# One more 128-column product ahead of each 256-column stretch of the feed-forwards

## The chip, the cores and the metric

The kernel runs on one core of a Trainium2 chip. The metric is the device time of one execution in microseconds, the median of several runs. TensorE (PE in the profile) multiplies; its weight loads have a row of their own (PEld). VectorE is DVE, ScalarE is ACT, GpSimd is POOL, and SyncE (SP) issues the large loads.

## What is computed

Two blocks over 256 tokens of width 1024, batch 1. The first has two layers (a gated mixer with a feed-forward, then an attention over compressed, selected and near tokens with a feed-forward); the second block has a gated linear attention with a convolution and a feed-forward with a convolution over a grid. Each has its own modulation from a condition. What bears on the change are the three feed-forwards:

```python
# first block, layers 0 and 1: ff_w_in is 1024 x 4096, ff_w_out 4096 x 1024
h = modulate(rms_norm(x, norm_g[layer, 2]), sh2, sc2)
y = jnp.square(jax.nn.relu(h @ ff_w_in[layer])) @ ff_w_out[layer]
x = x + g2[:, None, :] * rms_norm(y, norm_g[layer, 3])
...
# second block: w_up is 1024 x 5632, w_down 2816 x 1024
u, gate = jnp.split(h @ w_up, 2, axis=-1)
u = dwconv_grid(u, w_cf, b_cf, rows, width)
return (jax.nn.silu(u) * gate) @ w_down
```

All weights and activations are float32.

## The kernel before

The kernel is written engine by engine, with semaphores set by hand; the order of PE's work is the order of the calls in its program. Every weight matrix is streamed in chunks of 128 x 2048 float32 (1 MB) through a ring of six buffers (`raw`). A chunk is split into two tiles in the rounded float32 format: ACT writes the high part (`whi`, L724), DVE the rest (`wlo`, L1199), in rings of three. Activations are split the same way: `hh` and `hl` are the two halves of `hcat`. A product of the exact numbers is then three products of rounded ones: high by high, high by low and low by high. A rounded product is one record on PE; a product of plain float32 tiles (the full format) is two records, two passes. The trace writes f32 for both.

There are two kinds of stretches on PE in a feed-forward. `feature_major` (L1963) takes a chunk of 256 output features by 1024 inputs: for each half of 128 features and each of 8 slices of the inputs it issues the three products (L1971, L1972, L1973), the weights being the stationary operand and 256 tokens the moving one. That is 48 products of 256 columns into one bank; `linear_mid` (L2017) waits for the chunk (`split_ready`) and for the bank (`mid_free`) and calls it. `rows_onto_y` (L2056) takes a chunk of 256 rows of the output matrix: `tile_onto_y` (L2030) issues products with the activations stationary and 512 columns of the weights moving (L2039), 24 of them, into four banks that hold the sum over all chunks.

`ffn` (L2082) runs the two feed-forwards of the first block: first `ff_in(0)`, through `first_product`, which follows the normalised input slice by slice; then for c from 0 to 14 `ff_in(c + 1)` and, up to c = 13, `rows_onto_y` of chunk c; `end_of_y` ends it. In between stand a few products for the modulation (`ada_sum`, `ada_cols`, `ctx_transposes`, `ada_chunks`, `gain_row`). The last feed-forward has an up and a gate chunk in each step: `up(M_UP[c + 1])` and `up(M_GA[c + 1])`, 96 products of 256 columns, then `down(c)`, 24 products of 512. Other parts use `linear_mid` as well, the GLA part between products of the attention levels (L2520).

Each product has a weight load of its own, which PE can run while the product before it streams.

Of the kernel before, what the change touches and what calls it, by code (L numbers as in the profile page):

```python
# [11 lines left out]
P = 128  # L12
# [74 lines left out]
def build(nc, I, out, upto="ffn2"):  # L87
# [154 lines left out]
    if has("ffn2"):  # L242
# [3 lines left out]
        M_UP, M_GA, M_DN = [0] * CF, [0] * CF, [0] * CF  # L246
# [33 lines left out]
    hh, hl = hcat[:, :, 0, :], hcat[:, :, 1, :]  # L280
# [187 lines left out]
    ps = [banks[:, 512 * i:512 * i + 512] for i in range(8)]  # L468
# [9 lines left out]
    def sem(name):  # L478
        if name not in sems:
            sems[name] = nc.alloc_semaphore(name)  # L480
        return sems[name]

    raw_full = [sem(f"raw_full{i}") for i in range(RAW)]
    s_hi, s_lo, s_mm = sem("hi_ready"), sem("lo_ready"), sem("chunk_multiplied")
# [141 lines left out]
    with block:  # L626
# [1223 lines left out]
        def _(pe):  # L1850
# [106 lines left out]
            def w_of(m, kts=KT):  # L1957
                w = pl.width[m] // kts
                v = slice(0, pl.width[m])
                return (whi[:, m % SPL, v].rearrange("p (k n) -> p k n", n=w),  # L1960
                        wlo[:, m % SPL, v].rearrange("p (k n) -> p k n", n=w))

            def feature_major(m, bank, ah, al, between=None):  # L1963
                wh, wl = w_of(m)
                for nt in range(wh.shape[2] // P):
                    if nt and between is not None:
                        between()
                    dst = bank[:, T * nt:T * nt + T]
                    n = slice(nt * P, nt * P + P)
                    for kt in range(KT):  # L1970
                        pe.matmul(dst, wh[:, kt, n], ah[:, kt, :], start=kt == 0, stop=False)  # L1971
                        pe.matmul(dst, wh[:, kt, n], al[:, kt, :], start=False, stop=False)  # L1972
                        mm = pe.matmul(dst, wl[:, kt, n], ah[:, kt, :], start=False, stop=kt == KT - 1)  # L1973
                return mm
# [35 lines left out]
            def split_ready(m):  # L2010
                pe.wait_ge(s_lo, m + 1)
# [2 lines left out]
                if pl.last_use(pl.bank[u], u):  # L2014
                    pe.wait_ge(s_mid, pl.last_use(pl.bank[u], u))

            def linear_mid(m, ah, al, tm=False, o=None, between=None):  # L2017
                u = pl.um[m]
                split_ready(m)
                mid_free(u)  # L2020
                bank = ps[pl.bank[u]]
                if o is not None:
                    mm = first_product(m, bank, ah, al, o, tm)
                elif tm:
                    mm = token_major(m, bank, ah, al)
                else:
                    mm = feature_major(m, bank, ah, al, between)
                mm.then_inc(s_mm, 1)

            def tile_onto_y(m, ah, al, t, first=False):  # L2030
# [51 lines left out]
            def ffn(f, o, u, meanwhile=dummies, first=lambda: None):  # L2082
                m0, c0 = M_FF[f], 16 * f
                u0 = pl.um[m0]
                def ff_in(c, o=None):
                    linear_mid(m0 + (2 * c - 1 if c else 0), hh, hl, o=o)

                def squares(c):
                    pe.wait_ge(s_fact, c0 + c + 1)
                    at_ = lambda b: (lambda k, s: b[:, c % 3, T * k + s.start:T * k + s.stop])  # L2090
                    return at_(fhi), at_(flo)

                boundary(2 * f + 1, meanwhile, first)
                ff_in(0, o=o)
                if f == 1:
                    ada_cols(S2)
                for c in range(15):
                    if c == 14:

                        pe.wait_ge(s_gain, 2 * u + 1)  # L2100
                    ff_in(c + 1)
                    if ends_at(f, c - 1) is not None:
                        ada_sum(ends_at(f, c - 1))
                    if c + 1 in CTX_STEPS and f == 1 and has("gla"):
                        ctx_transposes(CTX_STEPS.index(c + 1))
                    if c >= 13:

                        pe.wait_ge(s_mid, u0 + c)
                        gain_row(u, c - 13)
                    if c < 14:  # L2110
                        rows_onto_y(m0 + 2 * c + 2, *squares(c), first=c == 0)
                        ada_chunks(FF_ADA[f][c])
                        if ends_at(f, c - 1) is not None:
                            ada_cols(ends_at(f, c - 1))

                def squares_ready():
                    pe.wait_ge(s_fact, c0 + 16)
                    if f == 1 and has("gla"):

                        pe.wait_ge(s_t, 8 * 6)  # L2120
                    ada_sum(ends_at(f, 14))

                r14 = squares(14)
                at_ = lambda b: (lambda k, s: b[:, 15 % 3, T * k + s.start:T * k + s.stop])
                end_of_y(m0 + 30, r14, (at_(fhi), at_(flo)), squares_ready, lambda: ada_cols(ends_at(f, 14)))
                ada_chunks(FF_ADA[f][14])
# [51 lines left out]
            if has("gmlp"):  # L2178
# [22 lines left out]
                for j in range(4):  # L2201
# [3 lines left out]
                    if j == 0:  # L2205
# [3 lines left out]
                        for b in range(2):  # L2209
                            for q in range(4):  # L2210
                                mm = pe.transpose(ps[b][:, q * P:q * P + P], ws[:, 4 * b + q, :], ident[:, :])
# [33 lines left out]
            if has("attn"):  # L2245
# [12 lines left out]
                for j in range(2):  # L2258
                    pe.wait_ge(s_blk, j + 1)
                    for c in range(2):  # L2260
                        m = M_CW[j][c]
                        split_ready(m)
                        wh, wl = w_of(m)
                        for i in range(8):
                            k = (8 * c + i) * WIN
                            ah, al = bw[j][:, k:k + P], bw[j][:, 16 * WIN + k:16 * WIN + k + P]
                            pe.matmul(ps[j][:, 0:T], ah, wh[:, i, :], start=c == 0 and i == 0, stop=False)
                            pe.matmul(ps[j][:, 0:T], ah, wl[:, i, :], start=False, stop=False)
                            mm = pe.matmul(ps[j][:, 0:T], al, wh[:, i, :], start=False, stop=c == 1 and i == 7)
                        mm.then_inc(s_mm, 1)  # L2270
                linear_mid(M_Q[1], hh, hl)
                for j in range(2):
                    pe.wait_ge(s_ht, j + 1)
                    for nt in range(2):
                        mm = pe.transpose(ps[2 + j][:, WIN * nt:WIN * nt + WIN], ht[:, j, P * nt:P * nt + P], ident[0:WIN, 0:WIN])
# [5 lines left out]
                wh, wl = w_of(M_GT)  # L2281
                for kt in range(KT):
# [3 lines left out]
                    mm = pe.matmul(dst, wl[:, kt, :], hh[:, kt, :], start=False, stop=kt == KT - 1)  # L2286
# [5 lines left out]
                for g in range(NG):  # L2292
                    for nt in range(2):
                        for i in range(2):
                            mm = pe.matmul(ps[1][32 * i:32 * i + NC, HD * g:HD * g + HD], hid[:, 1, nt, NC * g:NC * g + NC], w2v[:, nt, :],
                                           start=nt == 0, stop=nt == 1)
# [3 lines left out]
                for t in range(2):  # L2300
                    mm = pe.transpose(ps[4][:, 48 * t:48 * t + 48], gate_fm[:, P * t:P * t + P], ident[0:48, 0:48])
# [113 lines left out]
            if has("gla"):  # L2415
# [60 lines left out]
                for j in range(4):  # L2476
                    mm = pe.matmul(ps[2 + j // 2][:, T * (j % 2):T * (j % 2) + T], wab2[:, P * j:P * j + P], alx[:, :], start=True, stop=True)
# [16 lines left out]
                for f in range(2):  # L2494
                    for pair in range(GHD // 2):
                        for tt in range(2):
                            for h in (2 * pair, 2 * pair + 1):
                                dst = ps[2][64 * (h % 2):64 * (h % 2) + 64, 256 * f + P * pair:256 * f + P * pair + P]
                                mm = pe.matmul(dst, wc[:, tt, 256 * f + 64 * h:256 * f + 64 * h + 64], vctx[:, tt, P * h:P * h + P],
                                               start=tt == 0, stop=tt == 1)  # L2500
# [36 lines left out]
                for pair in range(GHD // 2):  # L2537
# [5 lines left out]
                    for h in (2 * pair, 2 * pair + 1):  # L2543
                        for it in range(2):
                            for jt in range(2):
                                a_ = (a_d if it == jt else a_x)[:, h % 2, jt, pair, :]
                                mm = pe.matmul(o_of(h)[:, P * it:P * it + P], vx[:, jt, P * h:P * h + P], a_, start=False, stop=it + jt == 2)
# [30 lines left out]
            if has("ffn2"):  # L2578
                def last_modulation(e):

                    pe.wait_ge(s_l4, 2)
                    pe.wait_ge(s_msr, 2)
                    ada_chunks(4)

                boundary(5, last_modulation)

                def up(m, bank, o=None):
                    split_ready(m)
                    if o is None:
                        feature_major(m, ps[bank], hh, hl).then_inc(s_mm, 1)  # L2590
                    else:
                        first_product(m, ps[bank], hh, hl, o).then_inc(s_mm, 1)

                def down(c):
                    pe.wait_ge(s_cact, c + 1)
                    at_ = lambda b: (lambda k, s: b[:, c % 2, T * k + s.start:T * k + s.stop])
                    if c < CF - 1:
                        rows_onto_y(M_DN[c], at_(chi), at_(clo), first=c == 0)
                    else:
                        last_rows_onto_y(M_DN[c], at_(chi), at_(clo))  # L2600

                up(M_UP[0], 6, o=7)
                ada_cols(G2B)
                up(M_GA[0], 4)
                for c in range(CF):
                    if c + 1 < CF:
                        if c:
                            pe.wait_ge(s_ue, c)
                        else:

                            ada_bank_free(G2B + 1)
                        up(M_UP[c + 1], 6 + (c + 1) % 2)
                        if c:
                            pe.wait_ge(s_fa, c)
                        up(M_GA[c + 1], 4 + (c + 1) % 2)
                    else:

                        pe.wait_ge(s_ue, c)
                        pe.wait_ge(s_fa, c)
                        gain_row(U_FF2, 0)  # L2620
                        gain_row(U_FF2, 1)
                    down(c)
# [119 lines left out]
```

## Time and profile before

| | |
|---|---|
| median of 3 runs | 1011.76 us (1010.94 to 1012.22) |
| the profiled execution | 1011.14 us |
| its span, first to last instruction | 1009.2 us |
| PE busy | 983.7 us, 6900 products |
| PE's weight loads busy | 865.8 us, 6901 loads |
| DVE busy | 801.6 us |
| ACT busy | 539.9 us |
| POOL busy | 77.4 us |
| read from HBM | 239.37 MB, 238 GB/s over the span |

A start is exact to the nanosecond in the records and printed to 0.01 us in the timeline. The end of a product is modelled, and products overlap: one of 256 columns is recorded as some 280 ns long though the next one starts well under 120 ns after it. So the pace of a stretch is read from the starts: the start of a product late in it less the start of an early one, by the number of steps between them. In the timeline neighbouring records of one line with the same operands are merged into one row (x2, x4).

### The profile page before, as it was taken

What the parts mean: (1) busy time and instruction counts of PE and PEld (TensorE: products, weight loads), DVE (VectorE), ACT (ScalarE), POOL (GpSimd) and SP (SyncE); (2) the same over time, 40 slices, a digit from 0 to 9 for tenths busy, and PEclk for the clock granted to TensorE, in tenths of its full rate; (3) what the DMA queues carried; (4) which work ended last, traced back from release to release, by engine and by line L of the source; (5) the groups of instructions that cost most, each with busy time, mean ns of one, the idle gap of its engine ahead of it and who ended that gap; (6) DMA issues with size and microseconds to landing.
All of it is one profiled execution on the core that took longest, in us unless ns stands there. A gap on an engine that the chain in (4) does not pass through costs nothing.

```text
span 1009.2 us, 16926 instructions
## 1 busy us (share of the span) xinstructions
PE 983.7 (97%) x6900; PEld 865.8 (86%) x6901; DVE 801.6 (79%) x1208; ACT 539.9 (53%) x706; POOL 77.4 (8%) x80
## 2 busy tenths in 40 slices
PE   6999999999999999999999999999999999999997
PEld 3687799989987989887889999988998889999996
DVE  2449799858988988877979778873799789888896
ACT  4354554444446547775545455464765765454544
POOL 0000000000000000000540000000791000000000
PEclk9999999999999999999999999999999999999999
DMA  9999699969997999002998877735433386555511
GB/s 340 387 384 375 224 337 393 349 225 358 351 338 255 287 365 353 2 2 84 377 372 299 282 269 286 255 95 167 127 132 127 119 282 220 186 189 190 186 43 42
DMA packets 130332, 243.60 MB, mean 241 GB/s; under 512 B 6586, under 2 KB 95311, under 8 KB 124111
## 3 DMA queue, kind: packets, MB, share of 16 engines
q1 hardware_dynamic: 125616, 238.77, 66.9%
q10 hardware_dynamic: 4639, 3.76, 1.4%
q8 instruction: 54, 0.88, 0.4%
q14 instruction: 23, 0.19, 0.1%
HBM read 239.37 MB, written 1.05 MB: 238 GB/s over the span
## 4 chain that ended last, share of the span: by engine, by line
PE 76%; DVE 6%; DMA 5%; POOL 4%; ACT 4%; SPq 2%; issue 2%; POOLq 0%; DVEq 0%; ACTq 0%
PE bank L2039 26%; PE bank L1971 11%; PE bank L1973 11%; PE bank L1972 11%; PE bank L2051 3%; DMA raw<-in_a_w_in_dram 3%; DVE wlo L1199 2%; DMA raw<-in_cmp_w_dram 1%; PE bank L2324 1%; PE bank L2350 1%; SPq L654 1%; DMA raw<-in_b_w_in_dram 1%; ACT whi L724 1%; PE bank L1865 1%; PE bank L2362 1%
## 5 line engine op out<-in xcount | busy, mean ns | idle before, releaser
L1199 DVE TENSOR_TENSOR wlo<-raw,whi 128x2048 fp32r<-128x2048 f32 x143 | 327.3, 2295 | 47.3 <-ACT whi L724 46.2
L724 ACT ACTIVATE whi<-raw 128x2048 fp32r<-128x2048 f32 x144 | 274.3, 1905 | 144.6 <-PE bank L2039 76.6
L1971 PE MATMUL bank<-hcat,whi 128*128 128x256 f32 x1096 | 309.1, 282 | 2.3 <-DVE wlo L1199 1.9
L1972 PE MATMUL bank<-hcat,whi 128*128 128x256 f32 x1096 | 307.0, 280 | 0.0
L1973 PE MATMUL bank<-hcat,wlo 128*128 128x256 f32 x1096 | 306.9, 280 | 0.0
L1971 PEld LDWEIGHTS bank<-hcat,whi 128*128 128x128 f32 x1096 | 206.0, 188 | 9.1 <-issue 3.5
L1973 PEld LDWEIGHTS bank<-hcat,wlo 128*128 128x128 f32 x1096 | 208.9, 191 | 0.0
L1972 PEld LDWEIGHTS bank<-hcat,whi 128*128 128x128 f32 x1096 | 206.0, 188 | 1.4
L1818 DVE SCALAR_TENSOR_TENSOR cvt<-ut,vec,cvt 128x189 f32<-128x189 f32 (+2 forms) x176 | 68.2, 429 | 19.3 <-ACT cvt L1162 16.8
L2039 PE MATMUL bank<-whi,fhi 128*128 128x512 f32 x240 | 74.7, 392 | 0.0
L2039 PE MATMUL bank<-wlo,fhi 128*128 128x512 f32 x240 | 74.0, 390 | 0.0
L2039 PE MATMUL bank<-whi,flo 128*128 128x512 f32 x240 | 74.0, 389 | 0.0
L859 ACT ACTIVATE fr<-bank 128x512 f32<-128x512 f32 x32 | 19.1, 598 | 95.4 <-PE bank L1973 91.3
L1237 DVE SCALAR_TENSOR_TENSOR acc_wide<-raw,csil,acc_wide 128x2048 f32<-128x2048 f32 x28 | 65.6, 2344 | 0.8
L2039 PEld LDWEIGHTS bank<-whi,flo 128*128 128x128 f32 x240 | 45.0, 188 | 9.5
L2039 PEld LDWEIGHTS bank<-wlo,fhi 128*128 128x128 f32 x240 | 45.0, 188 | 9.5
L2039 PEld LDWEIGHTS bank<-whi,fhi 128*128 128x128 f32 x240 | 43.1, 188 | 8.9 <-issue 1.7
L1865 PE MATMUL bank<-raw,cpad 128*32 128x512 f32 x256 | 32.7, 627 | 5.0 <-DMA raw<-in_ada_w_dram 4.8
L1493 DVE TENSOR_TENSOR fhi<-fr 128x512 fp32r<-128x512 f32 x32 | 22.3, 698 | 19.1 <-ACT fr L859 19.0
L805 ACT ACTIVATE t<-bank,mod,coef 128x256 f32<-128x256 f32 x64 | 30.4, 576 | 8.6 <-DVE coef L1366 5.2
L2039 PE MATMUL bank<-whi,hcat 128*128 128x512 f32 x112 | 32.4, 396 | 0.0
L1169 ACT ACTIVATE sl<-cvt 128x512 f32<-128x512 f32 x11 | 7.0, 633 | 34.6 <-DVE cvt L1818 34.6
(432 smaller groups left out, 1649.6 us busy)
## 6 DMA issues: line engine op xcount, KB each, us to landing
raw<-in_ada_w_dram SPq DMA_DIRECT2D x40, 1024.0 KB, 8.5
raw<-in_ff_w_in_dram SPq DMA_DIRECT2D x32, 1024.0 KB, 7.9
raw<-in_ff_w_out_dram SPq DMA_DIRECT2D x32, 1024.0 KB, 7.3
raw<-in_w_ada_dram SPq DMA_DIRECT2D x24, 1024.0 KB, 6.3
raw<-in_w_up_dram SPq DMA_DIRECT2D x22, 1024.0 KB, 5.1
raw<-in_w_in_dram SPq DMA_DIRECT2D x12, 1024.0 KB, 5.5
raw<-in_w_down_dram SPq DMA_DIRECT2D x11, 1024.0 KB, 4.9
raw<-in_ada_w_dram SPq DMA_DIRECT2D x16, 512.0 KB, 12.0
```

The lines of the kernel that those rows point to most:

```text
L724: act.activation(whi[:, m % SPL, 0:w], raw[:, pl.nm[m] % RAW, 0:w], ACT.Copy).then_inc(s_hi, 1)
L805: act.activation(t32[:, kt, :], ps[banks[kt // 2]][:, T * (kt % 2):T * (kt % 2) + T], ACT.Identity, scale=coef[:, c, kt:kt + 1], bias=mod[ ...
L1199: dve.tensor_tensor(wlo[:, m % SPL, 0:w], raw[:, pl.nm[m] % RAW, 0:w], whi[:, m % SPL, 0:w], ALU.subtract).then_inc(s_lo, 1)
L1237: ins = dve.scalar_tensor_tensor(out=to[:, :], in0=w, scalar=s, in1=to[:, :], op0=ALU.mult, op1=ALU.add)
L1493: dve.tensor_tensor(fhi[:, c % 3, :], fr[:, :], fr[:, :], ALU.mult).then_inc(s_fh, 1)
L1818: ins = dve.scalar_tensor_tensor(out=y, in0=grid(ut)[:, frm[0], frm[1]], scalar=vec[:, w_:w_ + 1], in1=y, op0=ALU.mult, op1=ALU.add)
L1865: mm = pe.matmul(ps[ADA_BANK][32 * g:32 * g + 32, :], cpad[:, c, k, :], w, start=i == 0, stop=i == CHUNKS[b] - 1)
L1971: pe.matmul(dst, wh[:, kt, n], ah[:, kt, :], start=kt == 0, stop=False)
L1972: pe.matmul(dst, wh[:, kt, n], al[:, kt, :], start=False, stop=False)
L1973: mm = pe.matmul(dst, wl[:, kt, n], ah[:, kt, :], start=False, stop=kt == KT - 1)
L2039: mm = pe.matmul(ps[2 * t + half][:, :], st_, w[:, k, n[half]], start=first and k + i == 0, stop=False, skip_group_check=True)
L2051: mm = pe.matmul(ps[2 * t + half][:, :], st_, w[:, k, n], start=False, stop=False, skip_group_check=True)
```

## The change

A function `offset_start` issues one product of the stretch's first weight tile with 128 columns of the high half of the activations, both in the rounded format, into the first 128 columns of the stretch's bank, as a product of its own (start and stop). The first product of the stretch starts its sum afresh over these columns, so the result isn't used. `feature_major` issues it, when asked to, ahead of its first product and behind the waits. It is asked to by `ff_in(c)` for c > 0 and by the up chunks 1 to 10; not by the first chunks, the gate chunks, nor by any other part.

```diff
+            def offset_start(bank, wh, ah):
+                pe.matmul(bank[:, 0:P], wh[:, 0, 0:P], ah[:, 0, 0:P], start=True, stop=True)
+
-            def feature_major(m, bank, ah, al, between=None):
+            def feature_major(m, bank, ah, al, between=None, offset=False):
                 wh, wl = w_of(m)
+                if offset:
+                    offset_start(bank, wh, ah)
                 for nt in range(wh.shape[2] // P):
...
-            def linear_mid(m, ah, al, tm=False, o=None, between=None):
+            def linear_mid(m, ah, al, tm=False, o=None, between=None, offset=False):
...
-                    mm = feature_major(m, bank, ah, al, between)
+                    mm = feature_major(m, bank, ah, al, between, offset)
...
-                    linear_mid(m0 + (2 * c - 1 if c else 0), hh, hl, o=o)
+                    linear_mid(m0 + (2 * c - 1 if c else 0), hh, hl, o=o, offset=c > 0)
...
-                def up(m, bank, o=None):
+                def up(m, bank, o=None, offset=False):
                     split_ready(m)
                     if o is None:
-                        feature_major(m, ps[bank], hh, hl).then_inc(s_mm, 1)
+                        feature_major(m, ps[bank], hh, hl, offset=offset).then_inc(s_mm, 1)
...
-                        up(M_UP[c + 1], 6 + (c + 1) % 2)
+                        up(M_UP[c + 1], 6 + (c + 1) % 2, offset=True)
```

## Rows read from the trace of the kernel before

**Rows 1.** The page: span, busy time by engine, chain that ended last by engine.

```profile
span 1009.2 us, 16926 instructions
...
PE 983.7 (97%) x6900; PEld 865.8 (86%) x6901; DVE 801.6 (79%) x1208; ACT 539.9 (53%) x706; POOL 77.4 (8%) x80
...
PE 76%; DVE 6%; DMA 5%; POOL 4%; ACT 4%; SPq 2%; issue 2%; POOLq 0%; DVEq 0%; ACTq 0%
```

**Rows 2.** Windows of the feed-forwards: us, busy PE PEld DVE ACT POOL, PEclk, DMA, GB/s.

```profile
131.33:295.34 164.01, 164.01 (x1077) 149.09 (x1075) 141.33 (x102) 73.42 (x61) 0.00 (x0) 1.00 0.93 337
489.79:654.84 165.05, 165.05 (x1083) 150.72 (x1083) 137.81 (x123) 79.24 (x78) 24.91 (x20) 1.00 0.84 302
828.29:990.34 162.05, 162.05 (x1179) 153.62 (x1177) 142.36 (x217) 81.88 (x79) 0.00 (x0) 1.00 0.49 168
```

**Rows 3.** Timeline of PE, one step, first feed-forward: start, length (us), line, operands.

```profile
153.56 0.28 PE L1971 MATMUL bank<-hcat,whi 128*128 128x256 f32 x1
...
159.21 0.62 PE L2039 MATMUL bank<-whi,fhi 128*128 128x512 f32 x2
...
164.65 0.28 PE L1971 MATMUL bank<-hcat,whi 128*128 128x256 f32 x1
```

**Rows 4.** Timeline of PE: an up and a gate chunk, and what follows.

```profile
845.06 0.28 PE L1971 MATMUL bank<-hcat,whi 128*128 128x256 f32 x1
...
856.37 0.39 PE L2039 MATMUL bank<-whi,chi 128*128 128x512 f32 x1
```

**Rows 5.** Timeline of PE, GLA: second and 48th product of a stretch.

```profile
744.15 0.29 PE L1972 MATMUL bank<-hcat,whi 128*128 128x256 f32 x1
...
749.38 0.28 PE L1973 MATMUL bank<-hcat,wlo 128*128 128x256 f32 x1
```

**Rows 6.** Windows (columns as in rows 2): that stretch.

```profile
744.15:749.38 5.23, 5.23 (x47) 5.23 (x47) 4.51 (x5) 3.13 (x3) 5.23 (x5) 1.00 0.45 165
```

**Rows 7.** Timeline of PE's weight loads: the first two of that stretch.

```profile
743.93 0.19 PEld L1971 LDWEIGHTS bank<-hcat,whi 128*128 128x128 f32 x1
744.04 0.19 PEld L1972 LDWEIGHTS bank<-hcat,whi 128*128 128x128 f32 x1
```

**Rows 8.** Chain of waits: start, us, what; 2-column products and 128-column transposes.

```profile
821.91 0.78 PE bank L1897 x7
...
222.35 0.44 PE bank L1899 x4
```

**Rows 9.** Timeline of PE, GLA: first of 50 512-column products, and what follows.

```profile
688.41 0.39 PE L2452 MATMUL bank<-whi,gcat 128*128 128x512 f32 x1
...
699.87 0.28 PE L2477 MATMUL bank<-alx,wab 98*128 98x256 f32 x1
```

**Rows 10.** Timeline of PE, first feed-forward: another 512-column stretch, and what follows.

```profile
228.28 0.63 PE L2039 MATMUL bank<-whi,fhi 128*128 128x512 f32 x2
...
233.77 0.28 PE L1971 MATMUL bank<-hcat,whi 128*128 128x256 f32 x1
```

**Rows 11.** Timelines of DVE and PE, second feed-forward: a low half, the stretch's first product.

```profile
600.82 2.29 DVE L1199 TENSOR_TENSOR wlo<-raw,whi 128x2048 fp32r<-128x2048 f32 x1 [1.04 <-ACT whi L724]
...
603.42 0.28 PE L1971 MATMUL bank<-hcat,whi 128*128 128x256 f32 x1
```

**Rows 12.** Timeline of PE ahead of GLA, where the order of operands changes.

```profile
676.46 0.28 PE L1985 MATMUL bank<-whi,gcat 128*128 128x256 f32 x1
...
677.40 0.28 PE L1987 MATMUL bank<-whi,gcat 128*128 128x256 f32 x1
...
677.76 0.28 PE L1998 MATMUL bank<-hcat,whi 128*128 128x256 f32 x1
...
679.34 0.28 PE L2007 MATMUL bank<-hcat,whi 128*128 128x256 f32 x1
```

**Rows 13.** Timeline of PE, last feed-forward, behind 2-column products: second product; first 512-column one.

```profile
822.75 0.28 PE L1972 MATMUL bank<-hcat,whi 128*128 128x256 f32 x1
...
839.60 0.63 PE L2039 MATMUL bank<-whi,chi 128*128 128x512 f32 x2
```

## The prediction

> **What bounds the kernel now.** I read the page first: TensorE (PE) is busy for 97% of a span of 1009.2 us, and the chain that ended last lies on it for 76%; DVE comes next with 79% busy, but only 6% of the chain [rows 1]. Then the three feed-forward parts by windows, from the first stretch that the change touches to the end of the last one: PE is busy for 164.01 of 164.01, 165.05 of 165.05 and 162.05 of 162.05 us. There is no idle time in them to win; only the pace of the products counts. The granted clock is 1.00 (the 2.4 GHz level) in all three, so the clock is not it either [rows 2].
>
> So I went to the timeline of PE and took start-to-start times. In a feed-forward step a stretch of 48 products of 256 columns (L1971 to L1973) runs from 153.56 to 159.21, then 24 products of 512 columns (L2039) to 164.65: 5.65 / 48 = 0.1177 us and 5.44 / 24 = 0.2267 us for one [rows 3]. In the last feed-forward the 96 products of an up and a gate chunk take 11.31 us, 0.1178 each [rows 4]. Now the same lines in the GLA part: from the second product at 744.15 to the 48th at 749.38 are 46 steps in 5.23 us, 0.1137 each [rows 5], at the same clock of 1.00 [rows 6]. The same three lines with the same operand shapes have two paces, and what differs is what ran ahead of the stretch. Every stretch that the change touches has the slow pace now; over a dozen stretches elsewhere, most of them behind a pause or behind products of another format, reach the fast one and keep it to their end. That is what the reader is to see: a stretch seems to inherit its pace from how it starts.
>
> **What the change does, and its price.** It adds 40 products: 15 in each of the two feed-forwards (c = 1 to 15) and 10 in the last (up chunks 1 to 10; the gate chunk behind each has none of its own). 35 of them stand right behind a 512-column product; the other five stand behind 256-column products or transposes. Each added product writes columns that the next product starts afresh, raises no semaphore and waits for nothing that the stretch does not wait for already. No DMA, ACT, DVE or POOL instruction is added, and no queue is passed. All of its time lies on PE, which has no idle time there [rows 2], so no cover hides any of it.
>
> No row shows a 128-column product in the rounded format, so I bound it. Below: its columns stream in half the time of 256, 0.1137 / 2 = 0.057 us [rows 5]. But its own weight load runs behind the last 512-column product, while the weight load of the next product can start only when it has started itself, and a weight load alone, with nothing streaming, takes from 743.93 to 744.04, 0.11 us [rows 7]. Products of 2 columns with fresh weights come at 0.78 / 7 = 0.111 us each, and full-format passes of 128 columns at 0.44 / 4 = 0.110 [rows 8]: the weight load is the floor, whatever the columns. Above: 0.118, if that load is slowed as in a slow stretch [rows 3]; and 0.22, if the product were run in two passes as a full-format one is, twice the 0.110 [rows 8]. I take 0.111, the row of short products with fresh weights: 40 x 0.111 = 4.4 us (2.3 to 4.7; with two passes 8.8).
>
> The Trainium skill ("TensorE: Matmul & The Clock Gate", section "Back-to-back issue gap") gives N / 2.4 + 2.5 ns for a product, 56 ns at 128 columns, which would make the 40 of them 2.2 us as an estimate. The same section says that in a stream of loads and products both set the spacing, and there the trace agrees: 2 columns cost as much as 128 [rows 8].
>
> **What it can give back.** If the added product puts a stretch at the fast pace, 48 products save 48 x (0.1177 - 0.1137) = 0.192 us and a pair of 96 saves 96 x (0.1178 - 0.1137) = 0.394 us [rows 3 to 5]; the 0.1137 has the slower first steps in it. 30 x 0.192 + 10 x 0.394 = 5.8 + 3.9 = 9.7 us.
>
> **What it may spoil.** The 512-column stretch behind has two paces as well. Behind fast 256-column products, from 688.41 to 699.87, 50 of them take 11.46 us, 0.2292 each [rows 9]: against 0.2267 that is 24 x 0.0025 = 0.06 us a step. Those are other operands; in the feed-forward the stretch at 228.28 starts out of step too and takes 5.49 us instead of 5.44 [rows 10], 0.05 more. Nothing is the other bound: all undisturbed stretches of this line run at 0.2267. I take the middle, 0.03 x 40 = 1.2 us (0 to 2.4).
>
> **What is late next.** The tightest product of DVE in these parts is the low half of the weights that ends at 600.82 + 2.29 = 603.11 for a stretch that starts at 603.42, 0.31 us ahead of it, and it is itself started from work that PE released [rows 11]. That chain runs beside the 512-column stretch, which does not get shorter; I put nothing for it. If its cover is gone a step gives back at most its own 0.08 us.
>
> Sum: 4.4 + 1.2 - 9.7 = -4.1 us. The profiled execution took 1011.14 us (1.9 us of it outside the span), the median of the runs is 1011.76, so it stands 0.62 below it; -4.1 makes 1007.0 on the one and 1007.7 on the other, and the second is my forecast.
>
> **Rivals.**
>
> *All 40 shift the pace* (the forecast, 0.53). For it: one hitch is enough elsewhere. From 676.46 to 677.40 8 products run at 0.1175; there the order of the operands changes, three steps take 0.36 us, 0.120 each, and from 677.76 to 679.34 14 run at 0.113 [rows 12]. A short product that leaves the stream waiting for a weight load is such a hitch. With 0.057 a product and nothing spoilt it gives -7.4 us, with 0.118 and 0.06 spoilt -2.6: 1004.4 to 1009.2.
>
> *No stretch shifts* (0.33), the case on the other side. The mechanism: the pace is set by how the weight loads fall against the streaming of the moving operand, and a start limited by a weight load brings back the same position. For it: behind the 2-column products at 822 the first product has to wait for its load in just this way, and the stretch settles at the slow pace all the same, 143 steps from 822.75 to 839.60 in 16.85 us, 0.1178 [rows 13]; all seven such starts behind full-format products do so, and the fast ones come mostly after a real pause of PE. Against it: those products are of another format, and the flip of [rows 12] needed no pause; so a third and not more. Then the 40 products are a pure cost at the first of the 256-column products: +4.4 us, 1016.2 (1014.1 to 1016.5). It decides where the start behind the added product leaves the second spacing at 0.118.
>
> The Trainium skill speaks for this outcome (same page, section "Step-by-step: what each phase is for"): loading the next tile's weights, it says, takes no read bandwidth from the running product, so a product of 256 columns would have one pace and there would be nothing to shift. The trace disagrees as far as the two paces go [rows 3, 5].
>
> *Some stretches shift* (0.12): the start falls at different positions from step to step, and half go fast. -4.9 + 4.4 + 0.6 = +0.1 us, 1011.9, with 2 us to either side for a quarter or three.
>
> *The added product runs in two passes, but the pace does shift* (0.02): 8.8 + 1.2 - 9.7 = +0.3 us, 1012.1.
>
> **How the numbers follow.** A difference under 0.2% (2.0 us) can't be told from none. Faster: the first case, 0.53. Slower: the second, 0.33. Within: the last two, 0.14. The likeliest time is 1007.7, its own range 1004.4 to 1009.2. The range to hold the time 8 times in 10 must take in the second case as well, for it has more than 2 in 10: 1005.0 to 1016.6.
>
> **What will show it.** Step by step in the changed kernel's timeline: the added record of 128 columns and the time from its start to the first L1971-like product (0.111 expected; 0.057 or 0.22 would show the bounds); the 48 products behind it in 5.46 us instead of 5.65, with a mean length in the grouped view that falls to that of the GLA stretches; the 512-column stretch at 5.44 to 5.50; still no idle time of PE in the three windows. I am wrong if the steps of the three lines stay at 0.1177, or if PE begins to wait for DVE's low halves.

## The result and the profile after

The changed kernel takes 1015.6 us, the median of 5 runs (1014.71 to 1017.02); the kernel before took 1010.97 beside it (5 runs, 1010.76 to 1012.22). The ratio is 1.0043, with an interval of 1.0032 to 1.0055: slower by 4.6 us, where 4.1 us less had been forecast. The profiled execution took 1014.71 us, 3.6 more than that of before.

The page of the changed kernel: span, busy time by engine, the chain that ended last.

```profile
span 1012.8 us, 17006 instructions
...
PE 985.5 (97%) x6940; PEld 868.0 (86%) x6941; DVE 801.0 (79%) x1208; ACT 539.7 (53%) x706; POOL 77.4 (8%) x80
...
PE 78%; DVE 6%; POOL 4%; DMA 4%; ACT 4%; issue 2%; SPq 1%; POOLq 0%; DVEq 0%; ACTq 0%
```

Against [rows 1] the span is 3.6 us longer, PE has 40 products more, and its part of the chain went from 76 to 78%. The same three windows as in [rows 2], same columns:

```profile
131.33:295.34 164.01, 164.01 (x1079) 148.95 (x1078) 140.71 (x102) 71.74 (x59) 0.00 (x0) 1.00 0.93 337
489.79:654.84 165.05, 165.01 (x1083) 150.15 (x1082) 137.18 (x124) 79.64 (x78) 25.32 (x20) 1.00 0.83 298
828.29:990.34 162.05, 162.05 (x1181) 153.49 (x1180) 141.63 (x215) 81.45 (x80) 0.00 (x0) 1.00 0.51 174
```

PE is busy as before (0.04 us of idle time in 165), the clock is 1.00 as before. Nothing new waits; PE has more to do and isn't faster. The timeline of PE in the first feed-forward, the step that answers to [rows 3] (L1964 is the added product, L1976 to L1978 were L1971 to L1973, L2044 was L2039):

```profile
163.22 0.62 PE L2044 MATMUL bank<-whi,flo 128*128 128x512 f32 x2
163.67 0.22 PE L1964 MATMUL bank<-hcat,whi 128*128 128x128 f32 x1
163.73 0.33 PE L1976 MATMUL bank<-hcat,whi 128*128 128x256 f32 x1
163.90 0.28 PE L1977 MATMUL bank<-hcat,whi 128*128 128x256 f32 x1
...
169.31 0.28 PE L1978 MATMUL bank<-hcat,wlo 128*128 128x256 f32 x1
169.43 0.63 PE L2044 MATMUL bank<-whi,fhi 128*128 128x512 f32 x2
...
174.90 0.22 PE L1964 MATMUL bank<-hcat,whi 128*128 128x128 f32 x1
```

The first 256-column product starts 0.06 us after the added one, but the second comes 0.17 behind it instead of 0.12. From the second at 163.90 to the 48th at 169.31 are 46 steps in 5.41 us, 0.1176 each: the pace of before. The 512-column stretch behind takes 174.90 - 169.43 = 5.47 us against 5.44 [rows 3]. PE's weight loads at this place:

```profile
163.44 0.19 PEld L1964 LDWEIGHTS bank<-hcat,whi 128*128 128x128 f32 x1
163.67 0.19 PEld L1976 LDWEIGHTS bank<-hcat,whi 128*128 128x128 f32 x1
163.78 0.19 PEld L1977 LDWEIGHTS bank<-hcat,whi 128*128 128x128 f32 x1
```

Loads start one behind the other: the short product doesn't shorten the 0.11 us from the first product's load to the second's (163.67, 163.78). In the records, exact to the nanosecond, the time from the last 512-column product to the first product behind the stretch is 5.991 us in the changed kernel and 5.880 before; for a pair of chunks 11.644 and 11.533. Both are 0.111 more. The grouped view of the whole first feed-forward (131.33 to 300 us; times x, busy us, mean ns of one) shows the pace unchanged: the mean lengths are 283, 280 and 280 ns, where the kernel before has 281 for each of the three lines.

```profile
L1976 PE MATMUL bank<-hcat,whi 128*128 128x256 f32 x237 | 67.2, 283 | 0.0
L1978 PE MATMUL bank<-hcat,wlo 128*128 128x256 f32 x238 | 66.8, 280 | 0.0
L1977 PE MATMUL bank<-hcat,whi 128*128 128x256 f32 x238 | 66.8, 280 | 0.0
```

All 35 places behind 512-column products kept 0.1178 us a product. Of the other five, four are at 0.1133. Two of these, c = 9 of the first and c = 5 of the second feed-forward, stand right behind four full-format transposes. PE's timeline of the first of them, its second and its 48th product, in the changed kernel and in the one before:

```profile
222.54 0.28 PE L1977 MATMUL bank<-hcat,whi 128*128 128x256 f32 x1
...
227.75 0.28 PE L1978 MATMUL bank<-hcat,wlo 128*128 128x256 f32 x1
```

```profile
222.75 0.28 PE L1972 MATMUL bank<-hcat,whi 128*128 128x256 f32 x1
...
228.16 0.28 PE L1973 MATMUL bank<-hcat,wlo 128*128 128x256 f32 x1
```

46 steps take 5.21 us, 0.1133 each, against 5.41, 0.1176. Both places are slow in all seven traces with nothing added there (before, runs 1 to 3 and 6 to 8), so at these two the added product did shift the pace. The other two, the first place of the first and of the last feed-forward, take either pace in those seven traces, and nothing can be said of them. The sum: 40 x 0.111 = 4.4 us, 24 undisturbed 512-column stretches with 0.023 each = 0.6, the four faster places -(3 x 0.2 + 0.4) = -1.0: +4.0 us, where 3.6 (profiled executions) and 4.6 (medians) were measured.

### The profile page after: what moved, and what is told of

Read it like the earlier page. It is cut to its first block, busy times and chain, and to the rows that moved or that the text cites. A ratio compares the mean times of both kernels' runs of the same rounds, so it can differ in the third digit from the quotient of the medians.

```text
span 1012.8 us, 17006 instructions
## 1 busy us (share of the span) xinstructions
PE 985.5 (97%) x6940; PEld 868.0 (86%) x6941; DVE 801.0 (79%) x1208; ACT 539.7 (53%) x706; POOL 77.4 (8%) x80
## 4 chain that ended last, share of the span: by engine, by line
PE 78%; DVE 6%; POOL 4%; DMA 4%; ACT 4%; issue 2%; SPq 1%; POOLq 0%; DVEq 0%; ACTq 0%
PE bank L2044 26%; PE bank L1976 11%; PE bank L1978 11%; PE bank L1977 11%; PE bank L2056 3%; DVE wlo L1199 2%; DMA raw<-in_a_w_in_dram 1%; DMA raw<-in_cmp_w_dram 1%; PE bank L2329 1%; PE bank L1865 1%; PE bank L2355 1%; DMA raw<-in_b_w_in_dram 1%; ACT whi L724 1%; SPq L654 1%; DVE hcat L1339 1%
## 5 line engine op out<-in xcount | busy, mean ns | idle before, releaser
L1976 PE MATMUL bank<-hcat,whi 128*128 128x256 f32 x1096 | 310.9, 284 | 2.5 <-DVE wlo L1199 1.7
L1978 PE MATMUL bank<-hcat,wlo 128*128 128x256 f32 x1096 | 306.9, 280 | 0.0
L1976 PEld LDWEIGHTS bank<-hcat,whi 128*128 128x128 f32 x1096 | 206.0, 188 | 9.0 <-issue 4.0
L1978 PEld LDWEIGHTS bank<-hcat,wlo 128*128 128x128 f32 x1096 | 205.9, 188 | 0.0
L2044 PE MATMUL bank<-whi,fhi 128*128 128x512 f32 x240 | 75.1, 394 | 0.0
L2044 PE MATMUL bank<-wlo,fhi 128*128 128x512 f32 x240 | 74.2, 390 | 0.0
L2044 PE MATMUL bank<-whi,flo 128*128 128x512 f32 x240 | 73.9, 389 | 0.0
L2044 PEld LDWEIGHTS bank<-wlo,fhi 128*128 128x128 f32 x240 | 45.1, 188 | 9.8
L2044 PEld LDWEIGHTS bank<-whi,flo 128*128 128x128 f32 x240 | 45.1, 188 | 9.7
L2044 PEld LDWEIGHTS bank<-whi,fhi 128*128 128x128 f32 x240 | 43.1, 188 | 8.9 <-issue 1.7
L2044 PE MATMUL bank<-whi,hcat 128*128 128x512 f32 x112 | 32.3, 396 | 0.0
```

The costliest lines, as they stand in the source:

```text
L2044: mm = pe.matmul(ps[2 * t + half][:, :], st_, w[:, k, n[half]], start=first and k + i == 0, stop=False, skip_group_check=True)
```

## The experiments

From the result on two theories stood against each other. *Position*: the start of a stretch against its first weight loads decides its pace, and 128 columns only happens to be a start that keeps the slow one. *History*: after a stream of rounded 512-column products a stretch is slow unless PE pauses or another format comes between; then no rounded product helps. In all runs "places" are stretches behind 512-column products; a stretch counts as fast at 0.1133 us a product, as slow at 0.1178. No pace in between settled in a stretch. In runs 1 to 5 the added product is L1969, the three products are L1997 to L1999 (L2035 in another order) and the 512-column ones L2101; in runs 6 to 8 these are L1971 to L1973 and L2045. The edits are shown in outline.

**1. Other widths**

```diff
-offset_start(bank, wh, ah)                    # 128 columns
+pe.matmul(bank[:, 0:n], wh[:, 0, 0:P], ah[:, 0, 0:n], start=True, stop=True)
```

At 35 places, with n from 16 to 256; most widths stand in two or three of the feed-forwards.

> The added product has another number of columns at each of 35 stretches that follow 512-column products: 16 to 256 in the first feed-forward, the same list backwards in the second, nine of them in the last. Theory A, the position of the start decides: some widths bring the stretch behind to 0.1133 us a product, others leave it at 0.1178, and a width does the same in both feed-forwards. Theory B, behind a stream of 512-column products in the rounded format no rounded product helps: all 35 stay at 0.1178. Either way the price is the weight load: start of the added product to the effective start of the next 0.107 to 0.112 us up to some 224 columns, 0.118 at 256, so 35 x 0.11 = 3.9 us more than before if none shifts (some 1015).

Measured: fast with 64, 80, 96 and 192 columns; slow with 16, 32, 48, 112, 144, 160, 176, 224, 240 and 256. The same width did the same in every feed-forward. 1011.66 us in one run (before: 1011.97). PE's timeline at two places, 96 columns and 176:

```profile
196.87 0.62 PE L2101 MATMUL bank<-whi,flo 128*128 128x512 f32 x2
197.32 0.21 PE L1969 MATMUL bank<-hcat,whi 128*128 128x96 f32 x1
197.36 0.35 PE L1997 MATMUL bank<-hcat,whi 128*128 128x256 f32 x1
197.55 0.28 PE L1998 MATMUL bank<-hcat,whi 128*128 128x256 f32 x1
...
202.88 0.39 PE L2101 MATMUL bank<-whi,fhi 128*128 128x512 f32 x1
...
255.17 0.62 PE L2101 MATMUL bank<-whi,flo 128*128 128x512 f32 x2
255.62 0.24 PE L1969 MATMUL bank<-hcat,whi 128*128 128x176 f32 x1
255.71 0.31 PE L1997 MATMUL bank<-hcat,whi 128*128 128x256 f32 x1
255.85 0.28 PE L1998 MATMUL bank<-hcat,whi 128*128 128x256 f32 x1
...
261.39 0.40 PE L2101 MATMUL bank<-whi,fhi 128*128 128x512 f32 x1
```

From the last pair of 512-column products to the next ones: 202.88 - 196.87 = 6.01 us and 261.39 - 255.17 = 6.22; the kernel before has 6.11 (5.880 + 0.227 from the records). So one rounded product can put a stretch at the fast pace, right behind 512-column products. History falls in its strict form; at these places the width decides, and not monotonically. All these products begin at column 0 of the bank and have the same weight tile, so only the number of columns differs.

**2. Other kinds of start**

Two and three products of 128 columns; products of another format; a wait of PE for the last product's end (a pause), alone and with a product; the low halves. At 35 places.

```diff
-offset_start(bank, wh, ah)
+for _ in range(2): offset_start(bank, wh, ah)      # or: three times
+pe.wait_ge(s_mm, m)                                # or: a pause of PE
```

> At the same 35 places different things stand ahead of the stretch: one, two or three rounded 128-column products, one of the low halves, one of bf16 with 64 to 512 columns, one in the full format with 128 or 32 columns, a full-format one with a rounded one behind it, a wait of PE for the end of its own 512-column products, and that wait with a rounded product. Theory A: shifts are scattered over the kinds, as the start happens to fall. Theory B: the waits and the full-format products, alone or with a rounded one behind, shift the stretch to 0.1133 (as four of the five places not behind 512-column products did in the changed kernel), the rounded and bf16 ones don't. A wait costs 0.2 to 0.3 us of idle PE, more than the 0.19 that a stretch can give back.

Measured: 1016.19 us in one run; from the last 512-column product to behind the stretch (5.880 with nothing, 5.991 with the one of the change):

| ahead of the stretch | us | pace |
|---|---|---|
| two of 128 columns | 5.898 | fast |
| three of 128 | 6.032 | fast |
| one of 128, of the low halves | 5.991 | slow |
| bfloat16, 64 or 128 | 6.004 | slow |
| bfloat16, 256 / 512 | 5.805 / 5.91 | fast |
| full format, 32 / 128 | 5.891 / 6.101 | fast / slow |
| full format 128 and rounded 128 | 6.018 | fast |
| a pause of PE | 6.269 | slow |
| a pause and one of 128 | 6.378 | slow |

The pause in the timeline of PE, then two products of 128 columns:

```profile
266.66 0.61 PE L2101 MATMUL bank<-whi,flo 128*128 128x512 f32 x2
267.42 0.36 PE L1997 MATMUL bank<-hcat,whi 128*128 128x256 f32 x1
267.62 0.28 PE L1998 MATMUL bank<-hcat,whi 128*128 128x256 f32 x1
...
273.04 0.28 PE L1999 MATMUL bank<-hcat,wlo 128*128 128x256 f32 x1
...
152.24 0.62 PE L2101 MATMUL bank<-whi,flo 128*128 128x512 f32 x2
152.69 0.33 PE L1969 MATMUL bank<-hcat,whi 128*128 128x128 f32 x2
152.86 0.33 PE L1997 MATMUL bank<-hcat,whi 128*128 128x256 f32 x1
153.03 0.28 PE L1998 MATMUL bank<-hcat,whi 128*128 128x256 f32 x1
...
158.25 0.28 PE L1999 MATMUL bank<-hcat,wlo 128*128 128x256 f32 x1
```

Behind the pause 46 steps take 273.04 - 267.62 = 5.42 us, 0.1178 each; behind two short products 158.25 - 153.03 = 5.22, 0.1135. A pause of this length doesn't bring the fast pace (and costs 0.39 us, more than the 0.2 to 0.3 expected); a second product of the change's own kind does. History is out; my reading of the fast stretches as "behind a pause" was one of circumstance.

**3. Other orders of the 48 products**

```diff
-for the two halves, for the 8 slices: high.high, high.low, low.high
+13 other orders (the three rotated and reversed, halves alternating, slices backwards, one kind after the other, two of a kind first)
```

> Nothing is added; at the 35 places the 48 products of a stretch stand in another order (13 orders: the three products of a slice permuted, the halves interleaved, slices backwards, all of one kind together, two of a kind first, as in the normalised first chunk, and so on). Theory A: the pace depends on how loads fall against the moving operand, so that some orders run at 0.1133 with no price (0.19 us a stretch, some 2 to 4 us in all if half of them do). Theory B: the pace comes from what ran before, so all orders stay at 0.1178 and the time is that of before, 1011.

Measured: 0.1178 and 5.880 us with every order; 1012.91 us in one run (before: 1011.97). Which operands follow each other in the stretch, and which comes first, changes neither the pace nor the price. The change that I had read from [rows 12] as the cause of a flip is another one, from moving weights to moving activations, which these orders don't test. But each of the 35 slow stretches of the kernel before has that change at its start, so it is no cause by itself.

**4. Two products of 128 columns at all 40 places**

```diff
 def offset_start(bank, wh, ah):
-    pe.matmul(bank[:, 0:P], wh[:, 0, 0:P], ah[:, 0, 0:P], start=True, stop=True)
+    for _ in range(2):
+        pe.matmul(bank[:, 0:P], wh[:, 0, 0:P], ah[:, 0, 0:P], start=True, stop=True)
```

> All 40 places of the change, with the 128-column product issued twice. If the price of a product is its weight load, the second adds 0.107 to 0.111 us: 40 x 0.11 = 4.4 us more than the changed kernel and 8.8 to 9.8 more than before (some 1020), where no pace shifts. Theory A: the second one moves the start once more, so the stretches behind 512-column products may go to 0.1133, and the time falls back by up to 9.7 us to some 1011. Theory B: none shifts.

Measured: all 40 stretches fast; 1010.65 us (10 runs, 1009.35 to 1012.11), ratio to the kernel before 0.9991 (0.9981 to 1.0). 5.898 us a stretch and 11.338 a pair (before 5.880 and 11.533), the 512-column stretch behind 0.015 more. The gain on which the forecast stood is real (5.991 + 0.111 = 6.102 would have been the slow stretch with two products; the fast one saves 0.204), but two products eat nearly all of it.

**5. 96 columns in place of 128, at all 40 places**

```diff
-    pe.matmul(bank[:, 0:P], wh[:, 0, 0:P], ah[:, 0, 0:P], start=True, stop=True)
+    pe.matmul(bank[:, 0:96], wh[:, 0, 0:P], ah[:, 0, 0:96], start=True, stop=True)
```

> The change with one size altered: 96 columns instead of 128 in all 40 added products. Theory A1, where the first product falls against its weight load sets the pace, and the number of columns moves it: with 96, as at six places of the run with many widths, the stretch goes to 0.1133. There the time from the last 512-column product to the end of a 48-product stretch was 5.792 us against 5.880 before, and 11.232 against 11.533 for a pair; the 512-column stretch behind took 0.015 more. So 30 x (0.088 - 0.015) + 10 x (0.301 - 0.015) = 2.2 + 2.9 = 5.0 us less than before: ratio 0.995. Rival A2, the shifts of that run came from the mixture of neighbours and don't hold when all places have the same: the stretches stay at 0.1178 and the time is that of the changed kernel, 4 to 5 us more than before, ratio 1.004.

Measured: 1007.29 us (5 runs, 1005.85 to 1008.86), ratio 0.9963 (0.995 to 0.9977). PE's timeline of the step at which the change was shown above:

```profile
163.13 0.62 PE L2101 MATMUL bank<-whi,flo 128*128 128x512 f32 x2
163.59 0.21 PE L1969 MATMUL bank<-hcat,whi 128*128 128x96 f32 x1
163.63 0.35 PE L1997 MATMUL bank<-hcat,whi 128*128 128x256 f32 x1
163.82 0.28 PE L1998 MATMUL bank<-hcat,whi 128*128 128x256 f32 x1
...
169.04 0.28 PE L1999 MATMUL bank<-hcat,wlo 128*128 128x256 f32 x1
169.15 0.63 PE L2101 MATMUL bank<-whi,fhi 128*128 128x512 f32 x2
```

From the second product to the 48th: 169.04 - 163.82 = 5.22 us, 0.1135 a step; the start to the next 512-column product is 6.02 us where the change has 169.43 - 163.22 = 6.21. The records: 5.792 and 11.232. All 35 places are fast and two of the other five; the three behind full-format transposes stayed slow, with the same 96 columns. They account for 0.6 us against the expectation; the profiled execution, which has them, took 1005.87 and meets it, so the 1.1 by which the median misses it lies within the scatter of the five runs. So the one number that decided between -4 and +5 us is the width of the added product: 32 columns fewer, in as many products.

**6. Nothing added, the last 512-column product cut in two**

```diff
-pe.matmul(ps[2 * t + half][:, :], st_, w[:, k, n[half]], ...)
+for a, b in ((0, 512 - w_), (512 - w_, 512)):       # the last product ahead of a stretch only
+    pe.matmul(ps[2 * t + half][:, a:b], st_, w[:, k, 512 * half + a:512 * half + b], ...)
```

At 35 places, with second pieces of 64 to 256 columns.

> Nothing is added: the last 512-column product ahead of 35 stretches is cut in two, the second piece 64 to 256 columns wide (the same list backwards in the second feed-forward, others in the last), so that all columns are used. Theory A1: the piece ahead of the stretch does what an added product of its width does, so pieces of 64 to 96 and of 192 columns give the fast pace, the others not; the price of the cut falls with its width, as the piece's columns had to stream anyway: 0.111 less 0.4427 ns a column, that is 0.07 us at 96, 0.03 at 192, none at 256. Rival A3: it is the stretch's distance from the end of a whole 512-column product that counts, and then a cut piece of the same width does otherwise than an added one, at other widths or none.

Measured: fast with 64, 112, 128, 144, 160, 176, 184, 200, 204, 212, 216, 220, 224, 240, 248 and 256 columns; slow with 80, 96, 192, 208 and 232. Again every width that stands at more than one place did the same at each. 1007.02 us in one run (before: 1011.15). From the last product that is whole (one ahead of the cut one) to behind the stretch, 6.107 uncut: 5.912 us (240) to 5.992 (64) where it is fast, 6.118 (232) to 6.175 (96) where it is slow. The widths that work here are others than those that work as an added product: 96 and 192 are now slow, 128 and 240 fast. It is not the width of the product ahead as such, then. Where it puts the start is what I take it to be, but none of these distances between starts in the traces separates fast from slow. With an added product (run 1, 16 to 240 columns) the second product of the stretch starts 0.455 to 0.461 us after the last 512-column one at either pace; with a cut the first starts 0.453 to 0.460 after the last whole one at either pace; and 160 columns put the second product 0.153 behind the first in both runs, slow as an added product and fast as a cut.

**7 and 8. Cuts of 240 and of 232 columns at all 35 places**

The edit of run 6, with second pieces of 240 columns in the one and 232 in the other.

> Nothing is added: at each of the 35 places behind 512-column products the last of these is cut into pieces of 272 and 240 columns, so the same columns are multiplied. If the start alone decides the pace, all 35 stretches take 0.1133 us a product. From the start of the product that is cut to the product behind the stretch that was 5.912 us in the trace of the mixed cuts, against 0.227 + 5.880 = 6.107 us uncut: 26 x 0.195 = 5.1 us. For a pair (cut of 220 columns) it was 11.358 against 0.227 + 11.533 = 11.760: 9 x 0.402 = 3.6 us. The 512-column stretches behind pay 0.015 each, 24 of them, 0.4 us. Sum 8.3 us less than before: 1002.8 us, +-1.3 for the stretches that start after a pause and differ from run to run. The rival, that a cut works where the neighbouring places are cut otherwise and not at every place, or that the time of the mixed cuts was a chance, gives 1007 to 1011 us.

> The same as the run before it with pieces of 280 and 232 columns: eight columns are moved from one piece to the other, the instructions are as many and the columns too. In the trace of the mixed cuts the stretch behind such a cut stayed at 0.1178 us a product and took 6.118 us from the start of the cut product, against 6.107 uncut. If the start alone decides, 35 x 0.011 = 0.4 us and 24 x 0.023 = 0.6 us on the 512-column stretches behind come on top: 1012.0 us, +-1.3, and about 9 us over the cut at 240. The rival, that one more, shorter product at these places is what helps, gives the same time as the cut at 240.

Measured: 240 gives 1002.3 us (5 runs, 1001.6 to 1004.18), ratio 0.9914 (0.9901 to 0.9928); 232 gives 1012.25 (10 runs, 1010.26 to 1014.13), ratio 1.0008 (0.9998 to 1.0017). (The expectation counts from "the cut product"; its numbers are from the whole one ahead of it, on both sides.) PE's timeline of one step with 240, the two pieces being merged into the x3 of the first row:

```profile
162.98 0.62 PE L2045 MATMUL bank<-whi,flo 128*128 128x512 f32 x3
163.44 0.28 PE L1971 MATMUL bank<-hcat,whi 128*128 128x256 f32 x1
...
168.78 0.28 PE L1973 MATMUL bank<-hcat,wlo 128*128 128x256 f32 x1
168.89 0.63 PE L2045 MATMUL bank<-whi,fhi 128*128 128x512 f32 x2
```

And with 232:

```profile
163.28 0.62 PE L2045 MATMUL bank<-whi,flo 128*128 128x512 f32 x3
163.73 0.29 PE L1971 MATMUL bank<-hcat,whi 128*128 128x256 f32 x1
...
169.28 0.28 PE L1973 MATMUL bank<-hcat,wlo 128*128 128x256 f32 x1
169.39 0.40 PE L2045 MATMUL bank<-whi,fhi 128*128 128x512 f32 x1
```

168.89 - 162.98 = 5.91 us against 169.39 - 163.28 = 6.11: the columns and the instructions are the same, and PE is busy throughout. The mean length of a record falls with the pace, to 277, 277 and 276 ns in the first feed-forward where the changed kernel had 283, 280 and 280:

```profile
L1972 PE MATMUL bank<-hcat,whi 128*128 128x256 f32 x239 | 66.1, 277 | 0.0
L1973 PE MATMUL bank<-hcat,wlo 128*128 128x256 f32 x239 | 66.0, 276 | 0.0
L1971 PE MATMUL bank<-hcat,whi 128*128 128x256 f32 x238 | 65.9, 277 | 0.0
```

Eight columns moved from one piece to the other are worth 10 us. This is the sharpest pair: the work is the same, and the records put 26 x 0.205 + 9 x 0.419 = 9.1 of the 10 us on the pace of the 35 stretches. (The second piece also begins at another column of bank and weights; run 1, where all begin at column 0, has both paces without that.) The cut at 240 beats both kernels, by 8.9 us the one before (medians 1002.3 and 1011.22) and by some 13 the changed one.

## Why the prediction was wrong, point by point

**What bounds the kernel** held: PE without idle time in the three windows, at a clock of 1.00, before and after. Apart from the pauses of run 2, the gains and losses of the eight runs lie in the pace of PE and the products added.

**The price of the added product** was right: 0.111 us, taken from the row of 2-column products with fresh weights [rows 8], and 0.111 measured, at single stretches and pairs alike. The bound of two passes did not come. The Trainium skill ("TensorE: Matmul & The Clock Gate", section "Back-to-back issue gap") has 56 ns for an isolated product of 128 columns, by which the 40 would have cost 2.2 us as an estimate, and says itself that this counts too little in a stream of loads and products, where it has about 81; with a fresh weight load for each the trace shows 111.

**The step that failed** is the condition of the third part, "If the added product puts a stretch at the fast pace", from which the 9.7 us were counted for all 40 places. At 35 of them, all those behind 512-column products, it doesn't: they stayed at 0.1178, the added products cost 0.111 each, and nothing was given back there. The two behind full-format transposes are the only ones that it is seen to shift. The evidence had been thin in a way that could be seen. I had two paces, and one event at which the slow one turned into the fast one [rows 12], and took from it that "one hitch is enough". The row against it stood in the text: starts limited by a weight load behind 2-column products that settle at the slow pace [rows 13]. I gave it a third, since those products are of another format. That row was no firmer: the first stretch behind those 2-column products, at which no run changes anything, is slow in five of the ten traces (before, changed, runs 2, 4 and 5) and fast in the other five. In each of the ten it has the other pace than the stretch ahead of the eight 2-column products, which take 0.696 us from first to last start behind a fast one and 0.700 or 0.701 behind a slow one. So the same start settles either way, and one trace could not show it. With one size of one product, unlike any start in the trace, the rows bore no more than even chances between all and none.

**The size of the gain** was right where a gain came: 0.192 a stretch and 0.394 a pair were forecast. Runs 5 and 1 show 5.991 - 5.792 = 0.199 and 11.644 - 11.232 = 0.412 for the same price; run 7, with nothing added, 0.195 and 0.41 against the kernel before. With 96 columns -3.9 us were measured, near the -4.1 of the forecast; that 96 is a width that works was in no row, so this is luck and no merit of the forecast.

**What it may spoil**: 0.03 a step was taken; 0.023 was measured behind a slow stretch with an added product and 0.015 behind a fast one (23 steps of the 512-column stretch: 5.236 and 5.228 us, 5.213 undisturbed).

**What is late next**: nothing, as forecast; also at 1002.3 us PE doesn't begin to wait for the low halves.

**The rival that came true** is the second, "No stretch shifts", at 1016.2 us; 1015.6 was measured. Its number held. Its mechanism, a start limited by a weight load that comes back to the same position, is not borne out: with 96 columns the loads of the first two products are 0.11 us apart as well, and the second product starts 0.456 us after the last 512-column one, as with 128, but those 35 stretches go fast. Shown by runs 1, 6, 7 and 8 is that what stands directly ahead decides: the same width does the same at every place behind 512-column products, and eight columns turn it. That it does so through the position of the start is argued and not shown. What makes one width fast and its neighbour slow stays open: the widths that work (64 to 96 and 192 added; 64, 112 to 184, 200, 204, 212 to 224 and 240 to 256 cut) follow no rule that I could find. The same page of the Trainium skill, section "Step-by-step: what each phase is for", says that the next tile's load takes no read bandwidth from the running product; the prediction took from it that a stretch would have one pace. Runs 7 and 8, with 10 us between them, show two; whether read bandwidth has a part in them no run here shows.

## What to carry to other kernels

Where a stream of small products with fresh weights bounds a kernel, read its pace from start to start at several places. If it has two, try several widths of the product just ahead, in one kernel with a different width at each place, since I found nothing in the trace that tells which will do. Cut a product that is there rather than add one: with fresh weights an added one costs the time of its weight load (0.111 us here), however few its columns, and a cut costs 0.01 to 0.07.

## What the runs showed of the hardware

Products of 128 x 128 weights with 256 moving columns in the rounded format run at one of two paces, 0.1133 and 0.1178 us each, at a granted clock of 1.00, and behind 512-column products keep it, from the sixth step at the latest, to the end of 48 or 96. None of 13 orders of the operands changed it, and a pause of PE left it slow at all the places where one was put.

Many stretches that start after a pause or behind products of other parts take one pace or the other from trace to trace. The stretch that starts at 65 us, ahead of which all ten kernels have the same instructions, is slow in four traces and fast in six. The six stretches of the GLA part between 719 and 757 us were all fast in run 5 and all slow in run 6, with the same instructions there. A stretch is worth 0.2 us, so the six differ by 1.2. That may be a part of the scatter between runs of one kernel, of which no two are traced here; and a single trace of a stretch at such a place says nothing about what was put ahead of it.
